# Hybrid decoder step on one core: 20 weight slots in the down products, weight sums and h sums on VectorE

## Chip, cores and metric

One core of a Trainium2 chip. The metric is the device time of one launch in microseconds, lower is better. Times are medians of runs on the chip.

## What is computed

One layer of a hybrid decoder: a prompt of 2048 tokens and 8 single tokens with a paged cache of 8192 past tokens. Attention and a state space model come first, then the gated feed-forward part, which is all that matters here:

```python
xn = rmsnorm(x, p['g_pre_ffn'])
gate = xn @ p['w_gate']                  # 1024 -> 2816
up = xn @ p['w_up']
padded = jnp.concatenate([conv_prev, gate], axis=1)
conv = p['conv_b'] + sum(padded[:, i:i + t] * cw[i] for i in range(3))
hdn = jax.nn.gelu(conv) * up
x = x + rmsnorm(hdn @ p['w_down'], p['g_post_ffn'])   # 2816 -> 1024
```

All values are float32.

## The kernel before, in words

The kernel runs its stages one after another; `stage_ffn` is the last. A float32 product is made of three products of rounded halves: ScalarE rounds an operand to its high part (`split`, `split_wd`, `split_a`), VectorE subtracts to get the low part, TensorE multiplies high by high, high by low and low by high. Large products are made by Strassen's scheme in Winograd's form: seven products (`OPS`, in the order K1, K6, K2, K7, K5, K4, K3) of sums of blocks instead of eight products of blocks.

**The gate loop** (`tiles`) has 44 tiles g: 22 blocks of 128 channels, first for tokens 0 to 1023, then for 1024 to 2047. A tile makes the gate and up values of one block from seven products of 12 matmuls of 128x512 (L2689). Around them in each tile: GpSimd makes four sums of weight blocks for the tile after (`prepare`: L1731, L1733, L1735; `finish`: L1737); ScalarE and VectorE split the seven weight operands of the next tile (L2786, L2938) as soon as TensorE has used the present one; ScalarE copies m1 and one result out of the banks (L2849, L2855) and makes the gelu of the tile before (L2797); VectorE adds the products up (L3025, L3030, L3033, L3036, L3039), makes the convolution (`taps`: L2995, L2998, L2999) and multiplies (L2964), which gives h. In the second half the 8 sample tokens are worked on as well, by small matmuls (L2703, L2711) and small instructions.

TensorE's waits in a tile: product K2 waits for m1 (L2849), K7 for L3025, K4 for L3030, K3 for L3033. All queues are in order, so an instruction that waits holds all that stands behind it on its engine.

The down products use Winograd's form too, so for each pair of tiles GpSimd makes five sums of the blocks of h (`sum_h`: L2594 four, L2596 one), in even tiles, and SyncE stores these and two raw blocks to DRAM (`hop`, L2417). In tiles 4 to 19 the even tiles also do a part of the sums of x for the second half: SyncE loads parts after it has stored h (`load_parts`, L2433), GpSimd makes four sums of them (`sum_parts`, L2605), SyncE stores those. GpSimd's order in an even tile g is: prepare(g+1), sum_h, sum_parts, finish(g+1).

**The down products** are 7 products i of 8 steps u, 56 steps s. A step is 11 x 3 matmuls of 128x512 into one of three banks (L2766): a block of h of 128 tokens (`a`, one 704 KB load, L2474, split by L2822 and L2957, two raw buffers) by the 11 weight operands of the product (`wd`, 16 slots of split operands in the memory of `xw`). A weight operand comes from one or two loads of 256 KB (L2462) into one of three raw slots (`NWD`), the two being added by GpSimd (`sum_wd`, L2638), and is split by L2814 and L2953. A raw slot is loaded again when VectorE has split what it held. Which blocks are loaded is in `PAIRED`; the first product takes two loads for each operand. The operands of product i+1 are loaded and split during the steps of product i, one per step in steps 1 to 5, three in step 6 and the rest in step 7 (`ops_of`). The weights of products 4 and 6 are also used raw for the 8 samples (`sample_down`, L2746), before they are added. Results are copied or added out of the banks by ScalarE (`evacuate`, L2892) and VectorE (`gather`, L3071), and in part copied on by GpSimd (L2665). During products 4 and 6 each step finishes a row of 128 tokens: square (L2900), norm on GpSimd (L2644, L2646), scaling and addition of x on VectorE (L3101, L3104), and the store of y by SyncE. SyncE's order in a step is: the load of h for two steps on, the weight loads, then the store of y, which waits for VectorE.

In the last gate tile (g = 43, `last`) the weight splits of the next tile are replaced by those of the first down product. Its loads start when all gate weights are split (after L2938's last) and the slots allow. Turns of the convolution's tails (L2724) stand behind the first six steps on TensorE.

## Time and profile before

| | us |
|---|---|
| median of 3 runs | 3459.91 (3459.48 to 3466.13) |
| profiled execution | 3459.59 |
| its span, first to last instruction | 3457.6 |
| mean granted clock of TensorE | 0.957 |
| TensorE matmuls busy | 3148.2 (91%) |
| VectorE busy | 2335.3 (68%) |
| ScalarE busy | 1323.6 (38%) |
| GpSimd busy | 1179.2 (34%) |

Busy times are sums over the whole span. Which engine sets the time differs by stage, so the rows that count are those of one stretch: `stage_ffn` begins its matmuls at 1936.9 us. In the trace PE is TensorE's matmuls and PEld its weight loads, DVE is VectorE, ACT ScalarE, POOL GpSimd, SPq the queue of SyncE's transfers. Tile names: `ahead_wf` and `ahead_S` are the raw gate weights and their sums, used again as raw buffers in the down products, `ahead_wop` the split gate weights and later the split h, `ffn_xw` the split x and later the split down weights, `gate_work` the working area of the gate loop, `down_C` the result.

### The profile page before, as it was taken

Reading aid. Unit: us, or ns where it says so; the run is one execution under the profiler, and the core shown is the slowest. Engines: PE = TensorE matmul, PEld = TensorE weight load, DVE = VectorE, ACT = ScalarE, POOL = GpSimd, SP = SyncE. Lnnn points to the kernel's source line nnn. Section 1 sums busy time; section 2 is a strip of 40 time slices with the busy share of each in tenths; the row PEclk is TensorE's granted clock in tenths of the full one; section 3 lists DMA queues with packets and bytes.
Section 4 is the critical chain, followed back from the end, with each engine's and each line's share of the span. In section 5 each row is a group of like instructions: output and inputs, shape, how many; then the busy total and the mean of one; then the engine's idle time right before and its main releaser. Section 6 shows DMA issues by size and latency. Waiting matters only on the chain. (4 is left out here: it accounts for less than half of the span.)

```text
span 3457.6 us, 47005 instructions
## 1 busy us (share of the span) xinstructions
PE 3148.2 (91%) x13945; PEld 2115.6 (61%) x13945; DVE 2335.3 (68%) x2904; ACT 1323.6 (38%) x2249; POOL 1179.2 (34%) x996
## 2 busy tenths in 40 slices
PE   6999985899999999998899599999899998899988
PEld 5787753344444444444787377777677776677666
DVE  6110678987988988994566676667888886344445
ACT  4100113666556556563444332223433332332222
POOL 2000101643444344341144345555355554122112
PEclk9999988999999999999999799999999999999999
DMA  3322234978988988997555233343433334454554
GB/s 116 101 79 67 76 87 118 304 235 281 304 277 284 305 273 288 306 298 242 181 164 151 88 107 105 110 115 109 143 92 96 97 98 126 148 177 163 175 192 167
DMA packets 501235, 591.69 MB, mean 171 GB/s; under 512 B 66191, under 2 KB 308975, under 8 KB 499372
## 3 DMA queue, kind: packets, MB, share of 16 engines
q1 hardware_dynamic: 494094, 574.17, 53.3%
q10 hardware_dynamic: 6912, 15.26, 1.4%
q8 instruction: 75, 1.23, 0.1%
q14 instruction: 122, 1.00, 0.1%
q0 software_dynamic: 32, 0.03, 0.0%
HBM read 484.37 MB, written 103.86 MB: 170 GB/s over the span
## 5 line engine op out<-in xcount | busy, mean ns | idle before, releaser
L2689 PE MATMUL tail_bank<-ffn_xw,ahead_wop 128*128 128x512 f32 x2112 | 530.4, 409 | 72.9 <-DVE ffn_xw L2943 31.6
L2689 PEld LDWEIGHTS tail_bank<-ffn_xw,ahead_wop 128*128 128x128 f32 x2112 | 408.1, 195 | 182.0 <-issue 50.3
L2766 PE MATMUL tail_bank<-ffn_xw,ahead_wop 128*128 128x512 f32 x1848 | 451.0, 405 | 20.8 <-DVE ahead_wop L2957 17.6
L1378 POOL TENSOR_TENSOR att_S<-att_S,att_X 128x512 f32<-128x512 f32 (+3 forms) x256 | 344.7, 1347 | 287.4 <-PE att_bank L1667 216.7
L2766 PEld LDWEIGHTS tail_bank<-ffn_xw,ahead_wop 128*128 128x128 f32 x1848 | 354.7, 193 | 121.1 <-DVE ahead_wop L2957 20.7
L2689 PE MATMUL tail_bank<-gate_xr,ahead_wop 128*128 128x512 f32 x1584 | 381.6, 399 | 16.2 <-DVE gate_work L3030 11.5
L2689 PEld LDWEIGHTS tail_bank<-gate_xr,ahead_wop 128*128 128x128 f32 x1584 | 300.4, 190 | 90.3 <-issue 18.1
L1562 DVE TENSOR_TENSOR att_prod<-att_Kr,att_q_wide 128x1024 f32<-128x1024 f32 x256 | 326.0, 1273 | 5.0 <-DMA att_Kr<-in_cache_k_dram 4.8
L1662 PE MATMUL att_bank<-att_X,att_negtri 128*128 128x512 f32 (+3 forms) x640 | 299.1, 550 | 29.4 <-DVE att_X L1533 28.7
L1567 DVE TENSOR_REDUCE att_z_s<-att_prod 128x16 f32<-128x1024 f32 x256 | 313.3, 1224 | 8.8
L1428 ACT ACTIVATE att_X<-att_bank 128x512 f32<-128x512 f32 (+2 forms) x320 | 171.0, 534 | 257.6 <-PE att_bank L1651 224.3
L1667 PE MATMUL att_bank<-att_S,att_negones 128*128 128x512 f32 (+3 forms) x576 | 259.3, 533 | 0.0
L2786 ACT ACTIVATE ahead_wop<-ahead_wf 128x512 fp32r<-128x512 f32 x215 | 135.2, 629 | 318.6 <-PE tail_bank L2689 218.6
L1436 ACT ACTIVATE att_Wt<-att_bank 128x512 f32<-128x512 f32 (+2 forms) x320 | 168.7, 527 | 128.3 <-PE att_bank L1667 128.0
L1533 DVE SCALAR_TENSOR_TENSOR att_X<-att_X,att_bank 128x512 f32<-128x512 f32 (+2 forms) x320 | 190.9, 598 | 29.7 <-ACT att_X L1430 28.7
L2938 DVE TENSOR_TENSOR ahead_wop<-ahead_wf,ahead_wop 128x512 fp32r<-128x512 f32 x215 | 179.5, 850 | 39.3 <-ACT ahead_wop L2786 37.6
L1374 POOL TENSOR_TENSOR att_S<-att_X,att_zero 128x128 f32<-128x128 f32 x120 | 100.2, 835 | 290.0 <-PE att_bank L1667 178.3
L1651 PEld LDWEIGHTS att_bank<-att_qhh,att_khl 128*128 128x128 f32 x320 | 61.1, 191 | 217.4 <-ACT att_Wt L1436 138.8
L1667 PEld LDWEIGHTS att_bank<-att_S,att_negones 128*128 128x128 f32 x576 | 112.2, 195 | 121.3 <-issue 106.5
L1430 ACT ACTIVATE att_X<-att_X 128x512 f32<-128x512 f32 (+2 forms) x320 | 181.3, 567 | 10.1
L2594 POOL TENSOR_TENSOR gate_work<-gate_work 128x512 f32<-128x512 f32 x88 | 129.1, 1495 | 138.0 <-DVE gate_work L2964 138.0
L1682 PE MATMUL att_bank<-att_Wt,att_vh 128*64 128x512 f32 (+3 forms) x640 | 161.1, 560 | 6.8 <-ACT att_Wt L1436 6.8
(416 smaller groups left out, 5495.9 us busy)
## 6 DMA issues: line engine op xcount, KB each, us to landing
att_Kr<-in_cache_k_dram SPq DMA_DIRECT2D x512, 256.0 KB, 3.7
att_Vr<-in_cache_v_dram SPq DMA_DIRECT2D x488, 256.0 KB, 3.8
hop_dram<-gate_work SPq DMA_DIRECT2D x154, 256.0 KB, 2.6
ahead_wf<-hop_dram SPq DMA_DIRECT2D x56, 704.0 KB, 4.4
ahead_wf<-in_w_gate_dram SPq DMA_DIRECT2D x44, 512.0 KB
ahead_wf<-in_w_up_dram SPq DMA_DIRECT2D x44, 512.0 KB, 5.3
ahead_S<-in_w_down_dram SPq DMA_DIRECT2D x45, 256.0 KB, 4.6
ahead_wf<-in_w_down_dram SPq DMA_DIRECT2D x45, 256.0 KB, 4.6
```

What stands on the lines that cost most here:

```text
L1378: pool.tensor_tensor(new[:, r:], old[:, r:], x[:, r:], ALU.add).then_inc(s_part, 1)
L1428: act.activation(x, bank[:, s % NZ, cols(s):], ACT.Exp).then_inc(e_ready, 1)
L1430: act.activation(x, x, ACT.Ln, bias=1.0).then_inc(l_ready, 1)
L1436: act.activation(Wt[:, u % NW, cols(u):], bank[:, u % NZ, cols(u):], ACT.Exp).then_inc(w_ready, 1)
L1533: stt(x, x, LN_TOP, z, ALU.min, ALU.max).then_inc(sp_ready, 1)
L1562: tt(pr, Kr[:, kk % KSLOTS], q_wide[:, None, :].to_broadcast([P, PP, AW]), ALU.mult).then_inc(k_used, 1)
L1567: dve.tensor_reduce(z_s[:, :, kk * PP:(kk + 1) * PP].rearrange("p h r -> p r h"), prod[:, kk % 2, :].rearrange("p (k h d) -> p k h d", k=P ...
L1662: last = pe.matmul(bank[:, u % NZ, o:], negtri[:], X[:, u % NX, o:], start=False, stop=True, skip_group_check=True)
L1667: last = pe.matmul(bank[:, u % NZ, o2:], negones[:], S[:, (u - 1) % 2, o2:], start=False, stop=True, skip_group_check=True)
L2689: mm = pe.matmul(bank[:, b, :], wop[:, k, w, q], xop(k, x)[:, q], start=(k in (K1, K6, K5) and q == 0 and n == 0), stop=(q == KH - 1 and n ...
L2766: mm = pe.matmul(bank[:, s % 3, :], a_op[s % 2][a][:, p, :], wd_op[:, n % NW, w, :], start=(p == 0 and q == 0), stop=(p == PAIRS_F - 1 and ...
L2938: tt(wop[:, k, 1], weight_part(early, k, s), wop[:, k, 0].bitcast(F32), ALU.subtract).then_inc(w_lo, 1)
```

## The change

All of it is in `stage_ffn` (and `ffn_ahead`, which makes its buffers).

- Memory that held rounded values only is now also seen as raw float32, so that each split weight slot is at the same time the two places of its raw loads: 20 slots (`NW`), loaded in place, summed in place, split in place. The three raw slots are gone. A slot is loaded again when TensorE has used it in the last step of its product.
- Blocks of h have three raw buffers (`NA`) instead of two. The third lies in memory of the gate loop's working area.
- Products 0 and 1 change places: the one with single loads comes first. ScalarE makes two copies of its result (before: one by ScalarE, one by GpSimd).
- The weight sums of the down products go from GpSimd to VectorE, at the end of each step's list. `LOADS`, `SUMS` and `SPLITS` say in which step each operand of the next product is loaded, summed and split.
- VectorE makes the five sums of h of a tile pair, two behind its K2 split and one each behind its splits of K7, K5 and K4; the last pair's stand behind the last multiplication.
- GpSimd makes L1737's sum (`finish`) before `sum_parts`.
- In the last gate tile the splits are placed anew, the first weight operand is loaded a tile earlier, 18 more as the slots come free.

```diff
...
+wd_op = ring_slots(stage_r, early["S_r"], early["wf_r"], xw, wop)
+wd_in = ring_slots(stage, S, wf, xw_raw, early["wop_raw"])
+NW = len(wd_op)
+XW0 = 3
+
+def wd_raw(n, h):
+
+    return wd_in[n % NW][:, 1 - h]
...
-PAIRED = {0: ((0, 1), (1, 1)), 1: ((1, 1),), 2: ((0, 0), (1, 1)), 3: ((1, 0), (0, 0)), 4: ((1, 0), (1, 1)), 5: ((0, 0),), 6: ((0, 0), (0, 1))}
-MINUS = (0, 3)
-NM = OPS * PAIRS_F
+PAIRED = {0: ((1, 1),), 1: ((0, 1), (1, 1)), 2: ((0, 0), (1, 1)), 3: ((1, 0), (0, 0)), 4: ((1, 0), (1, 1)), 5: ((0, 0),), 6: ((0, 0), (0, 1))}
+MINUS = (1, 3)
+LOADS = ((0, 1, 2), (3,), (4, 5), (6,), (7,), (8,), (), (9, 10))
+SUMS = ((), (0, 1), (2,), (3, 4), (5,), (6, 7), (8,), (9, 10))
+SPLITS = ((9, 10), (), (0, 1), (2,), (3, 4), (5,), (6, 7), (8,))
...
-    return range(o + u - 1, o + u) if 1 <= u <= 5 else range(o + 5, o + early_ones) if u == 6 else range(o + late_ones, o + PAIRS_F) if u == 7 else ()
-
-ACT_READS = (1, 1, 0, 1, 0, 0, 0)
+    return tuple((i + 1) * PAIRS_F + p for p in plan[u])
+
+ACT_READS = (2, 1, 0, 1, 0, 0, 0)
...
-            at(sp, wd_lo, n - NWD + 1)
+            if n >= NW:
+                i0, p0 = divmod(n - NW, PAIRS_F)
+                if p0 < PAIRS_F - 1:
+                    sp.wait_ge(wd_used, i0 * (PAIRS_F - 1) + p0 + 1)
+                else:
+                    sp.wait_ge(acc, (i0 + 1) * STEPS)
+            elif n >= XW0:
+                sp.wait_ge(prod, (LASTG - 1) * OPS + min((n - XW0) // 4 + 1 if n < NW - 1 else OPS, OPS))
+            elif n:
+                sp.wait_ge(w_lo, LASTG * OPS)
+                sp.wait_ge(s_made, FT)
+            else:
+                sp.wait_ge(x_ready[K3], 1 + KH)
...
-            at(sp, a_lo, s - 1)
             i, u = divmod(s, STEPS)
-            if s == 4:
-                sp.wait_ge(hraw_stored[0], 16 * 2 * PAIRS_F)
-                sp.wait_ge(hraw_stored[1], 16 * 2 * PAIRS_F)
-                for x in range(4):
-                    sp.wait_ge(hsum_stored[x], 16 * 2 * PAIRS_F * (2 if x == 0 else 1))
-            o = ((i * 2 + u // 4) * 4 + u % 4) * P
-            sp.dma_start(a_raw[s % 2], A["hop"][o:o + P, :]).then_inc(a_loaded[s % 2], 16)
-
-        def body(g):
-            if g < LASTG - 2:
-                weights(g + 2, (g + 2) % FT, g % 2)
-            if g == LASTG - 1:
+            if s < 2:
                 sp.wait_ge(w_lo, LASTG * OPS)
                 sp.wait_ge(s_made, FT)
-                sp.wait_ge(x_ready[K3], 1 + KH)
+            elif s == 2:
+                for done in (c11_ready, c21_ready, c12_ready, saved):
+                    sp.wait_ge(done, LASTG)
+                sp.wait_ge(tapped, LASTG * CW)
+            else:
+                sp.wait_ge(a_lo, s - NA + 1)
...
+            if g == LASTG - 2:
                 load_wd(0)
+            if g == LASTG - 1:
                 load_wd(1)
                 load_a(0)
                 load_wd(2)
                 load_a(1)
-                for n in range(NWD, PAIRS_F):
+                for n in range(XW0, NW - 1):
...
+        load_a(2)
+        load_a(3)
         store_h(LASTG, FT - 2, LASTG % 4, LASTG // 2)
-        sp.wait_ge(h_ready, LASTG)
...
-            if s + 2 < LASTS:
-                load_a(s + 2)
-            for n in ops_of(s, 8, 8):
-                load_wd(n)
+            if 4 <= s + NA < LASTS:
+                load_a(s + NA)
+            for n in ops_of(s, LOADS):
+                if n >= NW - 1:
+                    load_wd(n)
...
-            if j % 2 == 0 and not known(g, 0, 1):
-                sum_h(g, j, h2)
+            if not known(g, LASTG - 1):
+                finish(g + 1, (j + 1) % 2)
             if i is not None and j % 2 == 0:
                 sum_parts(i, j // 2)
-            if not known(g, LASTG - 1):
-                finish(g + 1, (j + 1) % 2)
...
-                    for n in ((0, 1), (2, 3), (4, 5), (6, 7), (8, 9), (10,), ())[k]:
+                    if k == K7:
+                        split_a(0)
+                    for n in ((0, 1), (2,), (3, 4), (5, 6), (7, 8), (9, 10), ())[k]:
                         split_wd(n)
-                    if k == K2:
-                        split_a(0)
-                    if k == K3:
+                    if k == K4:
...
-            dst = {0: C[:, 0, 1, u, :], 1: C[:, 0, 0, u, :], 3: C[:, 1, 0, u, :]}[i]
-            act.activation(dst, bank[:, s % 3, :], ACT.Copy, scale=-1.0 if i == 1 else 1.0).then_inc(c_act, 1)
+            for th, d, sign in {0: ((0, 1, 1.0), (0, 0, -1.0)), 1: ((1, 1, 1.0),), 3: ((1, 0, 1.0),)}[i]:
+                act.activation(C[:, th, d, u, :], bank[:, s % 3, :], ACT.Copy, scale=sign).then_inc(c_act, 1)
...
+        def sum_wd(n):
+
+            i, p = divmod(n, PAIRS_F)
+            if len(PAIRED[i]) == 1:
+                return
+            dve.wait_ge(wd_loaded[n % NW], wd_count(n))
+            if i in SAMPLED:
+                dve.wait_ge(sd_used, sampled_before(n))
+            tt(wd_raw(n, 0), wd_raw(n, 0), wd_raw(n, 1), ALU.subtract if i in MINUS else ALU.add).then_inc(wd_sum, 1)
...
+        def sum_h(g, j, h2, which):
+
+            if which:
+                dve.wait_ge(h_ready, g)
+            e, o = conv[:, (j - 2) % 4], conv[:, (j - 1) % 4]
+            for n in which:
+                x, a, b, op = ((0, e[:, 0:CH], o[:, 0:CH], ALU.add), (1, e[:, CH:], o[:, CH:], ALU.add),
+                               (2, e[:, 0:CH], o[:, CH:], ALU.add), (3, o[:, 0:CH], o[:, CH:], ALU.subtract),
+                               (0, e[:, CH:], e[:, 0:CH], ALU.subtract))[n]
+                at(dve, hsum_stored[x], h2 * 32 - (16 if n == 4 else 32) if x == 0 else h2 * 16 - 16)
+                tt(hsum[:, x, :], a, b, op).then_inc(hsummed, 1)
...
+                    if last:
+                        split_wd(9)
+                        split_wd(10)
+                        split_a(1)
                     taps(g, f, j, h2)
                 if not last:
                     split(g + 1, k, (j + 1) % 2)
                 else:
-                    for n in ((), (0, 1), (2, 3), (4, 5), (6, 7), (8, 9), (10,))[k]:
+                    for n in ((0,), (1, 2), (3,), (4,), (5, 6), (7, 8), ())[k]:
                         split_wd(n)
-                    if k == K7:
+                    if k == K5:
                         split_a(0)
-                    if k == K3:
-                        split_a(1)
                 if k == K6 and not known(g, 0, 1):
                     multiply(g - 1, (j - 1) % 4)
+                if j % 2 == 0 and not known(g, 0, 1):
+                    sum_h(g, j, h2, {K2: (0, 1), K7: (2,), K5: (3,), K4: (4,)}.get(k, ()))
...
+        sum_h(LASTG, LASTG % 4, LASTG // 2, range(5))
...
+            if s % STEPS == 0:
+                for n in ops_of(s, SPLITS):
+                    split_wd(n)
             if s and s + 1 < LASTS:
                 split_a(s + 1)
-            for n in ops_of(s, 0, 5):
-                split_wd(n)
+            if s % STEPS:
+                for n in ops_of(s, SPLITS):
+                    split_wd(n)
             if s and row_of(s - 1) is not None:
                 finish(s - 1)
+            for n in ops_of(s, SUMS):
+                sum_wd(n)
...
```

Lines with "..." stand for parts left out: the buffers' definitions, the same renaming of slots in other places, and the new places of waits that follow from the above.

## Rows read from the trace of the kernel before

**Rows 1.** Stretches: us; busy PE, PEld, DVE, ACT, POOL (xcount); granted clock; DMA share, GB/s
```profile
2060.00:2405.80 345.80, 317.93 (x1300) 253.07 (x1299) 239.34 (x279) 98.77 (x157) 181.37 (x133) 0.96 0.39 109
...
2470.00:2902.10 432.10, 432.10 (x2113) 338.27 (x2112) 356.69 (x470) 137.17 (x243) 223.98 (x134) 1.00 0.33 92
2902.10:2968.30 66.20, 42.91 (x159) 32.20 (x157) 29.54 (x33) 16.17 (x23) 22.54 (x17) 0.81 0.53 171
2968.30:3447.20 478.90, 453.59 (x1884) 345.90 (x1884) 218.54 (x217) 143.39 (x181) 88.64 (x83) 0.97 0.50 173
```

**Rows 2.** Waits, 2060 to 2405.8 us: total us, times, longest
```profile
ACT ahead_wop L2786 <- POOL ahead_wf L1737: 80.4, 8, 10.8
...
PE tail_bank L2689 <- ACT gate_work L2849: 27.9, 8, 4.3
```

**Rows 3.** Timeline, one tile pair of the gate loop: start, us, instruction [idle <-releaser]
```profile
2148.24 5.76 PE L2689 MATMUL tail_bank<-ffn_xw,ahead_wop 128*128 128x512 f32 x24
2157.20 7.42 PE L2689 MATMUL tail_bank<-ffn_xw,ahead_wop 128*128 128x512 f32 x24 [3.19 <-ACT gate_work L2849]
...
2145.46 1.97 SPq L2433 DMA_DIRECT2D ffn_stage<-xnT_dram  x4
...
2149.55 5.22 POOL L2605 TENSOR_TENSOR ffn_stage<-ffn_stage 128x256 f32<-128x256 f32 x4 [4.91 <-DMA ffn_stage<-xnT_dram]
2154.74 1.25 POOL L1737 TENSOR_TENSOR ahead_wf<-ahead_wf,ahead_S 128x512 f32<-128x512 f32 x1
...
2157.30 1.61 POOL L1733 TENSOR_TENSOR ahead_S<-ahead_S,ahead_wf 128x512 f32<-128x512 f32 x1
...
2159.56 1.04 ACT L2797 ACTIVATE gate_work<-gate_work 128x1024 f32<-128x1024 f32 x1
...
2146.31 0.69 DVE L2938 TENSOR_TENSOR ahead_wop<-ahead_wf,ahead_wop 128x512 fp32r<-128x512 f32 x1
...
2161.08 1.22 DVE L2964 TENSOR_TENSOR gate_work<-gate_work 128x1024 f32<-128x1024 f32 x1
```

**Rows 4.** Busy time: odd tile, next even tile, and a pair of the second half
```profile
2148.24:2172.85 24.61, 21.42 (x85) 16.87 (x84) 16.41 (x18) 6.23 (x10) 15.75 (x12) 0.93 0.25 72
2172.85:2192.50 19.65, 19.65 (x86) 15.87 (x85) 14.56 (x18) 6.36 (x10) 7.61 (x6) 1.00 0.59 163
...
2626.20:2668.60 42.40, 42.40 (x209) 33.20 (x208) 34.98 (x46) 13.56 (x24) 22.01 (x13) 1.00 0.34 93
```

**Rows 5.** Chain that ended last, in order: start, us, what
```profile
2959.14 6.12 DMA ahead_wf<-hop_dram
2965.28 1.39 ACT ahead_wop L2822
2966.69 1.64 DVE ahead_wop L2957
...
3003.28 69.31 PE tail_bank L2766 x297
...
3165.73 0.98 PE tail_bank L2746 x4
```

**Rows 6.** Timeline of the turn from gate to down products
```profile
2926.78 5.46 PE L2689 MATMUL tail_bank<-gate_xr,ahead_wop 128*128 128x512 f32 x12 [10.51 <-DVE gate_work L3030]
...
2967.18 1.02 PE L2724 MATMUL tail_bank<-kept_ident,ffn_tails 128*10 128x128 f32 x4 [7.38 <-ACT down_C L2911]
...
2911.44 1.30 POOL L2638 TENSOR_TENSOR ahead_S<-ahead_S 128x512 f32<-128x512 f32 x1 [10.56 <-DMA ahead_S<-in_w_down_dram]
```

**Rows 7.** Waits of the down products, 2968.3 to 3447.2 us
```profile
PE tail_bank L2766 <- DVE ahead_wop L2957: 17.6, 7, 4.4
```

**Rows 8.** Groups by line, second half: xcount | busy, mean ns | idle before
```profile
L2938 DVE TENSOR_TENSOR ahead_wop<-ahead_wf,ahead_wop 128x512 fp32r<-128x512 f32 x102 | 75.2, 752 | 1.2
L2594 POOL TENSOR_TENSOR gate_work<-gate_work 128x512 f32<-128x512 f32 x42 | 61.7, 1497 | 36.3 <-DVE gate_work L2964 36.3
```

**Rows 9.** Page, slices of the span: what the DMA moved
```profile
GB/s 116 101 79 67 76 87 118 304 235 281 304 277 284 305 273 288 306 298 242 181 164 151 88 107 105 110 115 109 143 92 96 97 98 126 148 177 163 175 192 167
```

More of the change, by code:

```diff
@@ L1708, in ffn_ahead @@
     m = Stage(nc, ctx, "ahead")
+    with ExitStack() as rounded:
+        mr = Stage(nc, rounded, "rounded")
+        wf_r = mr.far("wf", [P, 2, 4, KH, P], F32R)
+        S_r = mr.far("S", [P, 2, KH, P], F32R)
+        wop = mr.far("wop", [P, OPS, 2, KH, P], F32R)
     wf = m.far("wf", [P, 2, 4, KH, P])
     S = m.far("S", [P, 2, KH, P])
-    wop = m.far("wop", [P, OPS, 2, KH, P], F32R)
+    wop_raw = m.far("wop_raw", [P, OPS, 2, KH, P])
     prm = m.far("prm", [P, FT, ROWS])
@@ L2244, in stage_ffn @@
         st = m.sb("st", [P, 3, 2])
+        with ExitStack() as rounded:
+            mr = Stage(nc, rounded, "rounded")
+            stage_r = mr.sb("stage", [P, 2, CH], F32R)
+            xw = mr.sb("xw", [P, 4, 2, KH, CH], F32R)
         stage = m.sb("stage", [P, 2, CH])
-        xw = m.sb("xw", [P, 4, 2, KH, CH], F32R)
+        xw_raw = m.sb("xw_raw", [P, 4, 2, KH, CH])
         with ExitStack() as gates:
@@ L2266, in stage_ffn, with ring_slots @@
         raw = wf[:].rearrange("p s q k c -> p (s q k c)")
-        S_raw = S[:].rearrange("p s k c -> p s (k c)")
-        AW1 = PAIRS_F * P
-        a_raw = [raw[:, n * AW1:(n + 1) * AW1] for n in range(2)]
-        wd_raw = [S_raw, raw[:, 2 * AW1:2 * AW1 + 2 * CH].rearrange("p (s n) -> p s n", s=2), stage[:]]
-        NWD = len(wd_raw)
+        NA = 3
+        a_raw = [raw[:, 0:AW1], raw[:, AW1:2 * AW1], a_far[:]]
         ring = wop[:].rearrange("p o h k c -> p (o h k c)")
         a_op = [[ring[:, (2 * n + h) * AW1:(2 * n + h + 1) * AW1].rearrange("p (f t) -> p f t", t=P) for h in range(2)] for n in range(2)]
-        wd_op = xw[:].rearrange("p o h k n -> p (o h k n)").rearrange("p (w h n) -> p w h n", h=2, n=CH)
-        NW = 16
+        halves = lambda x: x.rearrange("p (h n) -> p h n", h=2)
+        def ring_slots(first, second, third, most, end):
+            flat = most[:].rearrange("p o h k n -> p (o h k n)")
+            return ([first[:], halves(second[:].rearrange("p s k c -> p (s k c)")),
+                     halves(third[:].rearrange("p s q k c -> p (s q k c)")[:, 2 * AW1:2 * AW1 + 2 * CH])]
+                    + [halves(flat[:, x * 2 * CH:(x + 1) * 2 * CH]) for x in range(16)]
+                    + [halves(end[:].rearrange("p o h k c -> p (o h k c)")[:, 4 * AW1:4 * AW1 + 2 * CH])])
+        wd_op = ring_slots(stage_r, early["S_r"], early["wf_r"], xw, wop)
[4 more added lines that the diff above has]
+            return wd_in[n % NW][:, 1 - h]
         def xop(k, h):
@@ L2382, in samples_of @@
         def samples_of(i, where):
-            return {**{u: (u - 2,) for u in range(2, 7)}, 7: (5, 6, 7), 8: (8, 9, 10)}.get(where, ()) if i + 1 in SAMPLED else ()
+            return ((), (0, 1), (2,), (3, 4), (5,), (6, 7), (8,), (), (9, 10))[where] if i + 1 in SAMPLED else ()
         def sampled_before(n):
@@ L2483, in body @@
+                    if s == 0:
                         for x in range(2):
@@ L2765, in _ @@
                         for q, (a, w) in enumerate(((0, 0), (0, 1), (1, 0))):
-                            mm = pe.matmul(bank[:, s % 3, :], a_op[s % 2][a][:, p, :], wd_op[:, n % NW, w, :], start=(p == 0 and q == 0),
+                            mm = pe.matmul(bank[:, s % 3, :], a_op[s % 2][a][:, p, :], wd_op[n % NW][:, w], start=(p == 0 and q == 0),
                                            stop=(p == PAIRS_F - 1 and q == 2), skip_group_check=True)
```

110 lines of the change are left out of this document (46 added, 64 removed).

## The prediction

> **What bounds the kernel now.** Everything the change touches lies in the last stage, from 1937 us on, so I read the busy times by stretch first [rows 1]. The second half of the gate loop is full: 432.1 us busy out of 432.1. TensorE sets its pace and nothing taken off another engine shortens it; an engine that becomes too full lengthens it. Time is lost in three places. The first half of the gate loop has 317.9 of 345.8 us busy, at a granted clock of 0.96. The turn from gate to down products takes 66.2 us with TensorE busy for 42.9. The down products take 478.9 us.
>
> **First place, the gate loop.** The waits say who is late [rows 2]: TensorE waits 27.9 us in 8 pieces for ScalarE's copy on L2849, and ScalarE stood 80.4 us in 8 pieces behind GpSimd's L1737, the fourth weight sum. The timeline of one of the eight tile pairs shows the path [rows 3]: GpSimd makes its sums of h, waits 4.9 us for the x parts that SyncE could only fetch after the last sum of h was stored, works on them for 5.2 us (L2605), and only then makes L1737, at 2154.7. ScalarE's queue is in order, so the copy of m1 behind it is late and TensorE stands for 3.19 us. That tile lasts 24.6 us against 19.65 us for the next one [rows 4]: 5.0 us lost, of which 1.8 us are slower matmuls, since the granted clock was 0.93 in that tile and 1.00 in the next; matmuls go at the lower of the two levels (1.2 instead of 2.4 GHz) for a while after the standstill.
>
> **Second place, the turn.** From 2902.1 to 2968.3 one gate tile (19.65 us) and two down steps are done. A down step is 69.31/9 = 7.70 us for 33 matmuls [rows 5], 8.05 with a turn of the tails, an estimate. 19.65 + 2 x 8.05 = 35.7, so 30.5 us are lost. The standstills are 10.51 us for L3030 on VectorE and 7.38 us near the end [rows 6]. Both come from three raw weight slots: each holds two loads, GpSimd adds them (first sum at 2911.4, after 10.56 us of waiting for the DMA), ScalarE and VectorE split them, and their own gate work stands behind those splits. The last chain [rows 5] is a late load of h: GpSimd's last sums of h, then 6.12 us of DMA, 1.39 and 1.64 us of splits.
>
> **Third place, the down products.** 54 steps x 7.70 = 415.8 us and 22 groups of sample products x 0.98 = 21.6 us [rows 5] make 437.4 of the 478.9 us [rows 1]; 41.5 us are lost. 17.6 us are standstills before the split of h (L2957), up to 4.4 us each [rows 7]; the rest is waits for weights, and matmuls slowed after these (granted clock 0.97).
>
> **The change, part by part.**
> *Sums of h on VectorE.* Removed from GpSimd: 5 per tile pair at 1.50 us [rows 8]. Added to VectorE: 5 at 0.69 to 0.75 us, taken from its split of the same size and operand count [rows 3, 8]; 3.5 to 3.8 us per pair. In a pair of the second half VectorE is busy 35.0 of 42.4 us [rows 4], so 7.4 us are free, and the five are spread over four places where it waits for TensorE. I cost them at nothing there; if that cover were gone they would be 22 x 3.8 = 84 us.
> *The fourth weight sum ahead of the x parts.* L1737 no longer waits behind L2605, so the wait of 3.19 us before K2 goes. What is late next: the sums of tile g+2, still behind L2605. The fifth sum of h now comes after VectorE's K4 split, which ends at 2147.0, so at 2147.7, and the x parts are asked for at about 2148.5 instead of 2145.5. L2605 ends near 2157.8 instead of 2154.8. Two weight sums more (2.9 us, the end of L1733 less the end of L1737) give 2160.8; ScalarE's split (0.63) and gelu (1.04), VectorE's product L2964 (1.22), its split (0.69) and the addition L3030 (0.69) follow in order and end near 2165.0. TensorE wants that addition for K4 at 2148.24 + 5 x 2.8 = 2162.2. So it stands about 2.5 us in a new place. With slower matmuls behind it I take 4.0 us per pair against 5.0: 8 x 1.0 = **8 us** gained. The ends are 0 and 5.0 us of loss per pair.
> *The turn.* The first down product now uses single loads that need no sum, 19 slots can be asked for during the last gate tile, and the first is asked for one tile earlier. 10 x 256 KB and 2 x 704 KB are 4.0 MB; the kernel got 171 GB/s on average in this stretch [rows 1], but with slots blocked. The highest slice of the whole span moved 308 GB/s [rows 9]; with requests close together I take that, 13 us, from 2907 to about 2921; at 171 GB/s it would be 24 us. By VectorE's order the splits, the gelu of tile 42 and its product then hold back K4 by about 2 us, and the first step begins near 2924 instead of 2940. Its two steps end near 2941. The third wants a block of h whose load waits for VectorE's last taps (2932): 6.1 us of DMA [rows 5], more behind the weights; and VectorE's five last sums now stand ahead of that split in its queue, the fifth waiting for the store of the first. I put the third step at 2945 against 2968.4: **23 us**. Ends: 15 and 30.5.
> *Down products.* The 55 weight sums cost GpSimd no time that shows; on VectorE they are 44 x 0.75 = 33 us beside 218.5 us busy in 478.9 [rows 1], 7 points more. What matters is order: a weight is asked for two steps ahead of its split, and a third slot for h takes L2957's loads off SyncE's stores of y. A split of h takes 1.39 + 1.64 us [rows 5] of a 7.70 us step. The standstills should go, all but sample groups, turns of the tails and a slow start after the turn; I leave 9.5 us: **32 us**. Ends: 15 and 41. The second copy out of the bank on ScalarE (0.6 us, 8 times, for GpSimd's copy) lies under a step.
>
> The sum is 8 + 23 + 32 = 63 us. The profiled execution took 3459.6 us (span 3457.6 and 2.0 around it), 0.3 us below the median of the runs, so this is 3459.6 - 63 = **3397 us** on either.
>
> **A rule against the change.** Splits on VectorE with two inputs from SBUF take 0.69 us in one tile [rows 3] and 0.75 us on average in the second half [rows 8]: little is lost there to GpSimd's sums. The Trainium skill ("SBUF — State Buffer", section "SBUF: two separate sides") says that such a VectorE instruction and a GpSimd instruction that reads SBUF exclude each other for the whole instruction. By that, every moved sum that meets a GpSimd sum costs its length more; what that would make of the time is rival 3. The average above agrees with it only if such meetings are rare or short.
>
> **The rivals.**
> 1. *The gate loop's standstill goes altogether*, if the x parts arrive as early as before or the chain to K4 is shorter: 8 x 5.0 = 40 instead of 8 us, 3365 us. For it: 2.5 us is a small margin. Against: L2605 still precedes the sums. 0.10.
> 2. *Half comes back*: VectorE, now with sums that wait for DMA and sample products in one in-order queue, holds TensorE at each of the six changes of product and in the turn. Half of 55 us: 3425 us. For it: this queue had no weight sums before. Against: it is under two thirds busy. 0.17.
> 3. *Slower: VectorE bounds the gate loop.* Price: a sum that meets a GpSimd sum costs 0.75 + 1.5 = 2.25 us, five are 11.2 us where 7.4 are free, 3.8 us over, x 22 = 84 us; 3397 + 84 = 3481 us. It decides from (7.4 + 63/22)/5 = 2.1 us per sum on. Against: GpSimd's own sums fall in a pair to 9 instead of 14 instructions, and the measured 0.75 us. 0.05.
> 4. *The change does not do what it says*: the turn and the down products are limited by the DMA, so that earlier requests end no earlier. Only the loop's 8 us stay: 3452 us. The DMA share of 0.50 to 0.53 [rows 1] speaks against it. 0.06.
>
> **How the numbers follow.** My forecast has 0.62, from 3382 to 3412 by its ends taken partly together. With half of rival 2 and most of the space to rival 1 the range is 3372 to 3425. 0.2% (7 us) is what a measurement can tell. Faster: all but rival 3 and stray mishaps, 0.93; same 0.02; slower 0.05.
>
> **What would show it.** Gate loop: TensorE's wait moves from L2849 to VectorE's L3030, 2 to 3 us, eight times; L1737 no longer waits behind L2605. Second half: still 432 us, all busy, VectorE near 90%. Turn: no 10.5 us standstill; the third step near 2937, as everything is 8 us earlier. Down: no waits over 2 us before L2957, clock 1.00 after the first steps. A second half above 435 us would make the prediction wrong on VectorE; a wait before weights at changes of product would be rival 2.

## The result, and the profile of the changed kernel

The median of four runs is **3365.3 us** (3362.5 to 3369.3) against 3459.7 for the kernel before on the same chip, a ratio of 0.9725 (95% interval 0.9708 to 0.9742): faster by 94 us. The prediction said faster, by 63 us, at 3397; its range ended at 3372, so the time lies 7 us outside, on the fast side. The profiled execution took 3369.3 us (span 3367.6) and is the longest of the four. Against the profiled execution of before that is 90 us less, and the stages ahead of the feed-forward part take 5.7 us more of it in this trace (its first matmuls start at 1942.6, before at 1936.9), so the last stage alone gains 95.7.

The stretches of the last stage, to be laid beside [rows 1] and [rows 4] (us; busy PE, PEld, DVE, ACT, POOL; granted clock; DMA share, GB/s): a tile pair of the gate loop's first half and its odd tile, the whole first half, the second half and one pair of it, the turn, the down products from their third step on.

```profile
2079.22:2120.43 41.21, 39.43 (x169) 31.50 (x169) 31.22 (x42) 12.36 (x20) 15.31 (x13) 1.00 0.44 122
2104.49:2125.90 21.41, 19.63 (x85) 15.56 (x84) 14.54 (x18) 6.01 (x10) 12.29 (x10) 1.00 0.40 111
2060.00:2405.80 345.80, 328.84 (x1415) 261.82 (x1413) 260.15 (x340) 101.51 (x165) 127.10 (x99) 1.00 0.43 120
2429.30:2880.30 451.00, 447.44 (x2184) 349.60 (x2185) 384.94 (x546) 145.40 (x258) 155.78 (x84) 1.00 0.34 95
2604.80:2647.20 42.40, 42.40 (x212) 33.16 (x208) 36.16 (x52) 13.48 (x25) 14.84 (x8) 1.00 0.34 93
2880.31:2922.36 42.05, 37.78 (x160) 29.64 (x158) 28.88 (x39) 17.91 (x26) 0.00 (x0) 0.96 0.81 279
2922.36:3357.04 434.68, 434.67 (x1884) 336.63 (x1884) 241.62 (x270) 140.97 (x186) 20.26 (x32) 1.00 0.56 189
```

With the same marks in both traces, the account of the last stage is:

| from | before, us | after, us | gained | predicted |
|---|---|---|---|---|
| first matmul to the first tile of the second half | 513.8 | 486.7 | 27.1 | 8 |
| from there to the last gate tile | 451.4 | 451.1 | 0.4 | 0 |
| last gate tile to the third down step | 66.3 | 42.1 | 24.2 | 23 |
| third down step to the last matmul | 478.8 | 434.7 | 44.1 | 32 |

The last matmul ends at 3357.0, the span 10.6 us later (before 10.4). Two terms stand out: the gate loop gave three times what was predicted, the down products 12 us more. In the rows above, the first half of the gate loop runs at a granted clock of 1.00, where before it was 0.96, and the down products have TensorE busy for all of their 434.7 us.

The waits of TensorE in the first half, beside [rows 2], say where the loop now waits: not on ScalarE's copy, but on VectorE's L3063, the addition before K4 (L3030 in the old lines).

```profile
ACT rounded_wop L2798 <- POOL ahead_S L1738: 60.0, 8, 7.5
...
PE tail_bank L2701 <- DVE gate_work L3063: 14.0, 8, 1.8
```

Eight waits, 14.0 us, 1.8 at most. The timeline of one pair, beside [rows 3] (start, us, instruction, idle before and its releaser), shows the path to one of them:

```profile
2104.64 1.96 SPq L2460 DMA_DIRECT2D ffn_stage<-xnT_dram  x4
...
2108.86 4.53 POOL L2642 TENSOR_TENSOR ffn_stage<-ffn_stage 128x256 f32<-128x256 f32 x4 [11.68 <-DMA ffn_stage<-xnT_dram]
...
2114.73 1.29 POOL L1738 TENSOR_TENSOR ahead_S<-ahead_S,ahead_wf 128x512 f32<-128x512 f32 x1
...
2116.13 0.63 ACT L2798 ACTIVATE rounded_wop<-ahead_S 128x512 fp32r<-128x512 f32 x1 [7.52 <-POOL ahead_S L1738]
2116.67 1.04 ACT L2809 ACTIVATE gate_work<-gate_work 128x1024 f32<-128x1024 f32 x1
...
2117.87 1.21 DVE L2985 TENSOR_TENSOR gate_work<-gate_work 128x1024 f32<-128x1024 f32 x1
...
2119.61 0.67 DVE L3063 TENSOR_TENSOR gate_work<-gate_work,tail_bank 128x512 f32<-128x512 f32 x1
...
2120.43 1.87 PE L2701 MATMUL tail_bank<-gate_xr,rounded_wop 128*128 128x512 f32 x7 [1.78 <-DVE gate_work L3063]
```

It is the chain that the prediction wrote down, link by link: x parts asked for late, GpSimd's four sums of them, two weight sums, ScalarE's split and gelu, VectorE's product and addition. The x parts take 4.53 us, not 5.22. It holds TensorE for 1.78 us where 2.5 were expected, and the matmuls behind it keep the clock: all eight groups of 24 take 5.83 or 5.84 us, where the 24 behind the old wait took 7.42 [rows 3].

The turn, beside [rows 6]:

```profile
2896.58 7.38 PE L2701 MATMUL tail_bank<-gate_xr,rounded_wop 128*128 128x512 f32 x24 [2.11 <-DVE gate_work L3063]
...
2922.36 0.97 PE L2778 MATMUL tail_bank<-rounded_stage,rounded_wop 128*128 128x512 f32 x3 [2.15 <-DVE rounded_wop L2978]
...
2913.38 2.50 DVE L2997 TENSOR_TENSOR gate_work<-gate_work 128x512 f32<-128x512 f32 x4
2920.07 0.69 DVE L2997 TENSOR_TENSOR gate_work<-gate_work 128x512 f32<-128x512 f32 x1 [4.19 <-DMA hop_dram<-gate_work]
2920.68 1.62 DVE L2978 TENSOR_TENSOR rounded_wop<-down_a_far,rounded_wop 128x1408 fp32r<-128x1408 f32 x1
```

The waits of 10.51 and 7.38 us are two of 2.1 us. The first of them, 2.11 us, is followed by the slower matmuls (24 in 7.38 us instead of 5.84; the stretch has a granted clock of 0.96), so in the turn this kernel does lose the clock, behind a wait only 0.3 us longer than those of the loop. The second is VectorE's split of h (L2978) behind its fifth sum of h, which waited 4.19 us for the store of the first. After that step TensorE has no wait in the down products at all [rows 7 of before had 17.6 us].

### The profile page after: what moved, and what is told of

It is laid out like the page before. It is cut to its first block and busy times, and to the rows that moved or that the text cites. A ratio compares the mean times of both kernels' runs of the same rounds, so it can differ in the third digit from the quotient of the medians.

```text
span 3367.6 us, 46986 instructions
## 1 busy us (share of the span) xinstructions
PE 3115.7 (93%) x13945; PEld 2096.1 (62%) x13945; DVE 2377.6 (71%) x3069; ACT 1320.8 (39%) x2257; POOL 931.9 (28%) x823
## 5 line engine op out<-in xcount | busy, mean ns | idle before, releaser
L2701 PE MATMUL tail_bank<-rounded_xw,rounded_wop 128*128 128x512 f32 x2112 | 515.4, 401 | 44.3 <-DVE rounded_xw L2954 31.4
L2701 PEld LDWEIGHTS tail_bank<-rounded_xw,rounded_wop 128*128 128x128 f32 x2112 | 398.6, 191 | 148.0 <-issue 50.1
L2701 PE MATMUL tail_bank<-gate_xr,rounded_wop 128*128 128x512 f32 x1584 | 380.8, 397 | 18.5 <-DVE gate_work L3063 17.2
L2778 PE MATMUL tail_bank<-rounded_xw,rounded_wop 128*128 128x512 f32 x1488 | 357.3, 396 | 0.0
L2701 PEld LDWEIGHTS tail_bank<-gate_xr,rounded_wop 128*128 128x128 f32 x1584 | 297.9, 189 | 94.4 <-DVE rounded_wop L2949 17.3
L2778 PEld LDWEIGHTS tail_bank<-rounded_xw,rounded_wop 128*128 128x128 f32 x1488 | 278.3, 188 | 77.9 <-issue 11.7
L2798 ACT ACTIVATE rounded_wop<-ahead_wf 128x512 fp32r<-128x512 f32 x215 | 134.2, 628 | 264.5 <-PE tail_bank L2701 235.7
L2949 DVE TENSOR_TENSOR rounded_wop<-ahead_wf,rounded_wop 128x512 fp32r<-128x512 f32 x215 | 157.3, 747 | 12.8 <-ACT rounded_wop L2798 11.4
L1651 PE MATMUL att_bank<-att_qhh,att_khl 128*128 128x512 f32 (+2 forms) x320 | 156.4, 489 | 1.4 <-ACT att_Wt L1436 0.8
```

The source lines that it names most:

```text
L1651: mm = pe.matmul(bank[:, s % NZ, o:], key[:, j * P:(j + 1) * P], part[:, c * CH + o:(c + 1) * CH], start=(q == 0), stop=(q == 1))
L2701: mm = pe.matmul(bank[:, b, :], wop[:, k, w, q], xop(k, x)[:, q], start=(k in (K1, K6, K5) and q == 0 and n == 0), stop=(q == KH - 1 and n ...
L2778: mm = pe.matmul(bank[:, s % 3, :], a_op[s % 2][a][:, p, :], wd_op[n % NW][:, w], start=(p == 0 and q == 0), stop=(p == PAIRS_F - 1 and q ...
```

## The experiments

Kernels e1 to e4 shared one chip, e5 to e8 another, e9 to e12 a third; ratios are to the kernel before on the same chip. Edits are to the changed kernel unless another is named. "Sums of h on GpSimd" are made there as in the kernel before. Line numbers shift by a few from one kernel to the next.

**Which part brings the gain.** The change mixes three things that touch the gate loop or the down products: the slots with all that belongs to them, the place of the sums of h, and the place of L1742 (L1737 in the old lines) before or after the x parts. The first three kernels take the combinations that the change left out.

e1_form_only, the slots and weight sums of the change, with sums of h and order as before:

```diff
-                    if not known(g, LASTG - 1):
-                        finish(g + 1, (j + 1) % 2)
+                    if j % 2 == 0 and not known(g, 0, 1):
+                        sum_h(g, j, h2)
                     if i is not None and j % 2 == 0:
                         sum_parts(i, j // 2)
+                    if not known(g, LASTG - 1):
+                        finish(g + 1, (j + 1) % 2)
...
-                        if j % 2 == 0 and not known(g, 0, 1):
-                            sum_h(g, j, h2, {K2: (0, 1), K7: (2,), K5: (3,), K4: (4,)}.get(k, ()))
```

> The changed kernel with GpSimd making the five sums of h again and L1737 again behind the work on the x parts (prepare, sums of h, x parts, L1737): only slots, weight sums and their placing are left of the change. Theory: the gate loop's share (27 us between the traces) hangs on these two edits alone, the turn's 24 us and the down products' 44 us do not. So the loop pair is 44.3 us again with the 3.2 us standstill on the copy of m1 and a granted clock under 1.00, and the time is 3365 + 26 = 3391 us. Rival: part of the loop's gain comes from the slots or the build as a whole; then under 3380.

Measured: 3386.8 us, ratio 0.9791 (0.9772 to 0.9809). e2_order_only, the same with `finish` ahead of `sum_parts`:

> As the run before, but with L1737 right behind GpSimd's sums of h and ahead of the x parts. Theory: the order alone takes the standstill away; with the sums on GpSimd the x parts are asked for some 3 us earlier than with the sums on VectorE, the weight sums of the tile after end some 3 us earlier, and the 1.76 us standstill before K4 is not there either: 8 x 1.76 = 14 us faster than the changed kernel, 3351 us, loop pair 39.2 us. Then moving the sums to VectorE costs time. Rival: the sums on VectorE are what pays; then the loop stands as before, 3391 us.

Measured: 3355.4 us, 0.9697 (0.9678 to 0.9716), below the changed kernel. e3_sums_only, the changed kernel with `finish` behind `sum_parts` again:

> The changed kernel with sums of h on VectorE, but L1737 again behind the x parts. Theory: the x parts come about 3 us later than with the sums on GpSimd and L1737 with them, so the standstill on the copy of m1 grows from 3.2 to about 6 us with slower matmuls behind it: 8 x 3 us slower than with both on GpSimd, 3415 us (3405 to 3425). Rival: GpSimd relieved of 7.2 us per pair makes L1737 in time; then 3365 to 3380 us.

Measured: 3410.1 us, 0.9859 (0.984 to 0.9878). The three rows of TensorE's waits in the first half (2060 to 2400 us), one of each kernel, tell why:

```profile
PE tail_bank L2715 <- ACT gate_work L2866: 28.4, 8, 4.3
```
```profile
PE tail_bank L2715 <- DVE gate_work L3077: 3.3, 8, 1.0
```
```profile
PE tail_bank L2701 <- ACT gate_work L2852: 38.3, 8, 4.9
```

e1 has the old wait on the copy of m1; e2, with the order alone, keeps 3.3 us of waits; e3, with the sums alone, has a longer wait on the copy than before, since the x parts are asked for after VectorE's last sum. So the order is what takes the loop's wait away. Moving the sums of h to VectorE costs 23 us without the order (e3 less e1). With it the cost is less sure: changed less e2 is 10 us, but the two were not run side by side, their intervals overlap, and the changed kernel once more (e12, below) had 0.9705, 0.0008 above e2. What speaks for a cost are the profiles: a pair of e2's loop lasts 40.2 us against 41.2, and its stretch from the last gate tile to the last matmul 472.3 against 476.7, together 8 + 4.4 us.

One after the other, by the ratios: slots, weight sums and placing alone gain 72 us (e1), the order 33 more (e2), and the sums of h take some 10 back, which leaves the 95 that the change has by its ratio. What within the 72 is due to the 20 slots, to the exchange of products 0 and 1 or to the places of loads and splits was not tried apart.

**The order alone, on the kernel before.** e9_before_order_only puts L1737 ahead of the x parts in the old kernel and changes nothing else:

```diff
                         sum_h(g, j, h2)
+                    if not known(g, LASTG - 1):
+                        finish(g + 1, (j + 1) % 2)
                     if i is not None and j % 2 == 0:
                         sum_parts(i, j // 2)
-                    if not known(g, LASTG - 1):
-                        finish(g + 1, (j + 1) % 2)
```

> The kernel before with one edit: L1737 right behind GpSimd's sums of h and ahead of the x parts. Theory: the loop's share does not hang on slots or on VectorE. The 3.2 us standstill goes, some tenths remain as in the form with this order (loop pair 40.2 instead of 44.3 us): 8 x 4.1 = 33 us faster, 3427 us, ratio 0.990. Rival: the gain needs the relieved GpSimd; then no change.

Measured: 3430.1 us, 0.9904 (0.9883 to 0.9926), 33 us by the ratio. So 33 of 94 us are to be had by moving one call. Its waits, beside [rows 2]:

```profile
PE tail_bank L2689 <- DVE gate_work L3030: 3.3, 8, 1.0
PE tail_bank L2689 <- DVE gate_work L3025: 1.5, 7, 0.3
```

**How long a standstill the clock bears.** My forecast had 2.5 us with slower matmuls behind them; the trace has 1.78 at full clock. To see whether the length alone decides, GpSimd makes one more sum of weights of the odd tiles, between its x parts and L1736: half a block in e5, a whole one in e6, so that the same chain ends later.

```diff
+                    if i is not None and j % 2 == 1:
+                        pool.wait_ge(w_lo, g * OPS + K5 + 1)
...
+                        tt(S[:, 0, 0:2], wfx[:, A21, 0:2], wfx[:, A22, 0:2], ALU.add).then_inc(dup, 1)
+                        pool.wait_ge(dup, i * 2 - 1 + j // 2)
                     if not known(g, LASTG - 1):
                         prepare(g + 1, (j + 1) % 2, h2 + j % 2)
```

> The changed kernel with one more GpSimd instruction of 128x256 ahead of the sums that the K4 standstill hangs on, in the eight tile pairs. It lengthens that standstill from 1.76 to about 2.4 us, near the 2.5 us of the prediction. Theory: below the 3.2 us of the kernel before TensorE's clock is not lowered, so only the wait itself is added: 8 x 0.65 = 5 us, 3370 us, granted clock 1.00 in the loop. Rival: 2.4 us is enough, as the prediction took it; then each pair loses 1.7 us more, 3384 us, clock 0.96.

> The same with 128x512: the standstill grows to about 3.05 us. Theory: near enough to 3.2 us that the clock falls for a while in most pairs, 8 x (1.3 + 1.7) = 24 us, 3389 us. Rival: the clock holds, 3376 us.

Measured: e5 3383.3 us, 0.9775 (0.9758 to 0.9791); e6 3391.5 us, 0.9798 (0.9782 to 0.9815). Two neighbouring waits of e5, and one of e6 (24 matmuls after each wait):

```profile
2164.15 7.38 PE L2709 MATMUL tail_bank<-gate_xr,rounded_wop 128*128 128x512 f32 x24 [2.66 <-DVE gate_work L3071]
2207.79 5.84 PE L2709 MATMUL tail_bank<-gate_xr,rounded_wop 128*128 128x512 f32 x24 [2.66 <-DVE gate_work L3071]
```
```profile
2159.47 7.38 PE L2709 MATMUL tail_bank<-gate_xr,rounded_wop 128*128 128x512 f32 x24 [3.22 <-DVE gate_work L3071]
```

The same 24 matmuls last 5.84 us at full clock and 7.38 when it falls. In e5 the waits are 2.66 to 2.99 us and five of the eight are followed by the longer time; in e6 they are 3.22 to 3.48 and all eight are. In the loop of the changed kernel, at 1.72 to 1.78 us, none is, nor in its repetition e12; in e4 and in e8, both below, one of eight each, at 1.79. Between 1.8 and 2.1 us there are single waits only: 1.88 us in e2's turn and 2.06 in e8's loop are not followed by the longer time, 1.93 in e3's turn, 1.99 in e1's and 2.11 in the changed kernel's are; in e12 this wait of the turn is 1.75 us and the time 5.83. So e5's theory, that only the wait is added (3370 us), was wrong, and its rival's 3384 came out.

A pair of e5 lasts 42.98 us on average over seven, one of the changed kernel 41.18: 1.8 us more per pair, 0.9 of it wait and the rest slower matmuls. That is 14 us for eight pairs; e5 less changed is 18 us by the medians, not run side by side. Two full tiles are 39.3 us (2 x 19.65), so e5 loses 3.7 us per pair, where the prediction took 4.0 for a wait of 2.5 us. Its price was about right for its wait; the wait was not there.

**Does VectorE have room?** e7_sums_twice makes each sum of h twice on VectorE, 3.45 us more per pair where 6.2 us look idle in a pair of the second half.

```diff
+                        tt(hsum[:, x, :], a, b, op).then_inc(dup, 1)
+                        dve.wait_ge(dup, h2 * 5 - 4 + n)
                         tt(hsum[:, x, :], a, b, op).then_inc(hsummed, 1)
```

> The changed kernel with each of VectorE's five sums of h made twice: 3.45 us more per tile pair. Theory: VectorE still has room (36.2 of 42.4 us busy in a pair of the second half), so the second half stays full and the time grows only where a sum is on the path: the fifth sum and with it the x parts come 0.7 us later in eight pairs, and some in the turn, 3370 to 3380 us. Rival (the prediction's third): VectorE bounds the gate loop; then TensorE stands in the second half and the time is over 3400 us.

Measured: 3427.0 us, 0.9901 (0.9885 to 0.9918). I had expected no loss in the second half; this missed by 50 us. A pair there, in the windows view; then TensorE's three waits in it, and one doubled sum (L2998 and L3000) beside GpSimd's:

```profile
2624.11:2669.17 45.06, 43.01 (x209) 33.09 (x209) 39.37 (x57) 13.55 (x24) 14.51 (x8) 1.00 0.32 88
```
```profile
2624.11 1.07 PE L2716 MATMUL tail_bank<-ahead_wf,ffn_xs 128*32 128x256 f32 x16 [1.49 <-DVE ffn_hs L3097]
...
2661.32 3.04 PE L2702 MATMUL tail_bank<-gate_xr,rounded_wop 128*128 128x512 f32 x12 [0.27 <-DVE gate_work L3066]
2664.64 3.04 PE L2702 MATMUL tail_bank<-gate_xr,rounded_wop 128*128 128x512 f32 x12 [0.28 <-DVE gate_work L3069]
```
```profile
2656.86 0.68 DVE L2998 TENSOR_TENSOR gate_work<-gate_work 128x512 f32<-128x512 f32 x1
2657.01 1.69 POOL L1742 TENSOR_TENSOR ahead_wf<-ahead_wf,ahead_S 128x512 f32<-128x512 f32 x1 [4.24 <-DVE rounded_wop L2950]
2657.57 1.68 DVE L3000 TENSOR_TENSOR gate_work<-gate_work 128x512 f32<-128x512 f32 x1
```

A pair takes 45.06 us instead of 42.40 while VectorE is busy for 39.4, and all three waits of TensorE, 2.0 us together, are for VectorE. So here VectorE's queue sets the pace at 87% busy. My reading is that its idle time lies ahead of instructions that wait for TensorE, so that work added in other places pushes back what TensorE waits for; that was not tried by moving the added sums elsewhere. In any case the 6 us of idle time were no measure of what could be added.

**Weight sums of the down products.** e4_wd_on_gpsimd makes them on GpSimd, all else as changed:

```diff
                     if s and row_of(s - 1) is not None:
                         finish(s - 1)
-                    for n in ops_of(s, SUMS):
-                        sum_wd(n)
...
                         norm(row_of(s - 1))
+                    for n in ops_of(s, SUMS):
+                        sum_wd(n)
```

> The changed kernel with the weight sums of the down products on GpSimd, slots and steps unchanged. Theory: slots and distance make the gain, not the engine: the sums have two steps of room, so 3365 us within 5. Rival: GpSimd's sums (1.3 us and more against 0.7) and its norms in one queue bring waits for weights back; then 3375 us or more, with standstills in the steps of products 4 and 6.

Measured: 3374.6 us, 0.9751 (0.9733 to 0.9768). In the profiles the last gate tile to the last matmul takes 481.8 us against 476.7, and nearly all of the difference (4.8 of 5.1 us) lies in the turn; from the third step on e4 has no wait either. So 3374.6 came out at the rival's time, but not by its mechanism, standstills in products 4 and 6. The turn's timeline:

```profile
2903.78 11.23 POOL L2672 TENSOR_TENSOR ffn_xw_raw<-ffn_xw_raw 128x512 f32<-128x512 f32 x6 [1.06 <-DMA ffn_xw_raw<-in_w_down_dram]
...
2906.08 2.71 DVE L2980 TENSOR_TENSOR rounded_wop<-ahead_wf,rounded_wop 128x1408 fp32r<-128x1408 f32 x1
...
2911.73 4.36 DVE L3033 SCALAR_TENSOR_TENSOR gate_work<-gate_work,ahead_prm 128x1024 f32<-128x1024 f32 x2
...
2916.22 1.02 PE L2748 MATMUL tail_bank<-kept_ident,ffn_tails 128*10 128x128 f32 x4 [7.03 <-DVE ffn_tails L3034]
```

In the changed kernel, where GpSimd does nothing in this stretch, the split of h takes 1.62 us and the two taps 2.60:

```profile
2905.81 1.62 DVE L2978 TENSOR_TENSOR rounded_wop<-ahead_wf,rounded_wop 128x1408 fp32r<-128x1408 f32 x1
...
2908.40 2.60 DVE L3031 SCALAR_TENSOR_TENSOR gate_work<-gate_work,ahead_prm 128x1024 f32<-128x1024 f32 x2
```

Six sums of GpSimd side by side with VectorE's last taps make both slower (1.87 us each for GpSimd's, 1.3 elsewhere), and TensorE waits 7.0 us for the tails. By the rule that the prediction weighed (the Trainium skill, "SBUF — State Buffer", section "SBUF: two separate sides"), a VectorE instruction with two inputs from SBUF and a GpSimd instruction that reads SBUF exclude each other for the length of an instruction. These rows fit it: 2.71 and 4.36 us against 1.62 and 2.60, which is 1.1 us more for the split and 0.9 for each tap, beside sums of 1.3 to 1.9 us.

**The third buffer of h.** e8_two_h_buffers sets `NA = 2` and drops the waits for the third buffer's memory.

```diff
-        NA = 3
+        NA = 2
```

> The changed kernel with two raw buffers for blocks of h instead of three. Theory: the gain of the down products comes from weights asked for two steps ahead, and with these no load waits long in SyncE's queue, so the third buffer is worth under 5 us: 3360 to 3370 us (the third block comes earlier in the turn, since it no longer waits for the taps: up to 2 us of gain). Rival: it is the third buffer that takes the loads of h off the stores of y; then the 12 us of standstills of product 4 return, 3378 us or more.

Measured: 3369.5 us (3362.0 to 3376.0), 0.9739 (0.9721 to 0.9757): no difference that could be told. The third buffer is worth nothing that shows here; with two, the profile has no wait before the third step and the down products run as full. With e4, where GpSimd makes the weight sums and they run as full too, this leaves the slots and the placing of loads and splits as what fills the down products: an argument by elimination.

**Can the rest of the loop's wait be had?** The x parts are asked for behind the stores of h, which now wait for VectorE's last sum. In e10 and e11 SyncE asks for them ahead of these stores; e11 has the sums of h on GpSimd as e2.

```diff
+                            load_parts(i, j // 2)
                             store_h(i * 4 + j, None, j, i * 2 + j // 2)
-                            load_parts(i, j // 2)
```

> The changed kernel with SyncE asking for the x parts ahead of its stores of h. Theory: what is left in the loop is GpSimd's work on the x parts standing ahead of the next tile's sums because the parts come late; asked for early it is done in the even tile, and the 1.76 us standstill goes: 8 x 1.76 = 14 us, 3351 us. Rival: it then runs beside VectorE's sums of h and holds these up; then 3358 us or more, with new waits in the even tiles.

> Slots and order of the change, sums of h on GpSimd (as the second run), and the x parts asked for ahead of the stores of h. Theory: the last 0.5 us of standstill and the slowed instructions per pair go, loop pair 39.2 us: 8 x 1.0 = 8 us faster than the second run, 3347 us, about 3% under the kernel before. Rival: GpSimd is full in these tiles, nothing changes, 3355 us.

e12_changed_again is the changed kernel on that chip:

> The changed kernel once more, beside the other three on the same chip: 3365 us, ratio 0.9725. By the theory the second run's form is 0.0028 below it, which is then no difference between chips.

Measured: e12 3363.6 us, 0.9705 (0.9687 to 0.9723); e10 3356.0 us, 0.9677 (0.9658 to 0.9696), 7.6 less than e12, where the theory had 14 and the rival 7 at most; e11 3364.2 us, 0.971 (0.9689 to 0.973), where 3347 was expected. In e10 a pair lasts 39.9 us against 41.2:

```profile
2070.86:2110.72 39.86, 39.43 (x168) 31.50 (x169) 32.62 (x42) 12.98 (x21) 15.36 (x12) 1.00 0.44 126
```

In e11 it lasts 41.0, though its chain over the x parts is gone. Its timeline:

```profile
2140.44 1.74 POOL L1736 TENSOR_TENSOR ahead_S<-ahead_wf 128x512 f32<-128x512 f32 x1
2141.17 4.32 DVE L3045 SCALAR_TENSOR_TENSOR gate_work<-gate_work,ahead_prm 128x1024 f32<-128x1024 f32 x2
...
2142.25 2.16 POOL L1738 TENSOR_TENSOR ahead_S<-ahead_S,ahead_wf 128x512 f32<-128x512 f32 x1
2144.49 2.15 POOL L1740 TENSOR_TENSOR ahead_wf<-ahead_wf 128x512 f32<-128x512 f32 x1
2145.41 1.26 DVE L3046 TENSOR_SCALAR ffn_tails<-gate_work 128x2 f32 x1
...
2147.78 0.68 DVE L3072 TENSOR_TENSOR gate_work<-gate_work,tail_bank 128x512 f32<-128x512 f32 x1
2148.61 3.03 PE L2715 MATMUL tail_bank<-rounded_xw,rounded_wop 128*128 128x512 f32 x12 [1.63 <-DVE gate_work L3072]
...
2162.15 2.71 DVE L3045 SCALAR_TENSOR_TENSOR gate_work<-gate_work,ahead_prm 128x1024 f32<-128x1024 f32 x2
```

GpSimd, free earlier, makes its three weight sums exactly while VectorE makes its taps: 4.32 us instead of the 2.71 of the next tile, the small instruction behind them takes 1.26 us, the addition before K7 is late, and TensorE waits 1.6 us. As the timeline reads, the gain of one wait was paid for by a collision that had not been there; e11 equals e12 on the same chip. In e10 the same three sums lie ahead of the taps, which VectorE, with its sums of h, begins later:

```profile
2142.89 1.62 POOL L1740 TENSOR_TENSOR ahead_wf<-ahead_wf 128x512 f32<-128x512 f32 x1
```
```profile
2145.87 2.71 DVE L3031 SCALAR_TENSOR_TENSOR gate_work<-gate_work,ahead_prm 128x1024 f32<-128x1024 f32 x2
```

The last of them ends at 2144.5, and the taps take their 2.71 us.

The best versions are e2 (3355.4 us, 0.9697) and e10 (3356.0, 0.9677); the changed kernel had 0.9725 and 0.9705. All five runs of e10 are shorter than all five of e12 on the same chip. The intervals of the ratios overlap, and no run of the changed kernel stands beside e2; the profiles show the shorter pairs in both.

## Why the prediction was wrong in size, and where it was right

- **Right: what bounds the three places, and that all three open.** Signs, causes and the new last links were as written: L3030's addition in the loop, the fifth sum before the split of h in the turn, nothing in the second half (0.4 us).
- **The step that failed: "With slower matmuls behind it I take 4.0 us per pair against 5.0".** The new wait was sized 2.5 us and priced as one at which the clock falls. It is 1.78 us at a granted clock of 1.00. A pair lasts 41.2 us, before 44.3 (24.61 + 19.65, [rows 4]) to 44.4 in other pairs: 3.2 us per pair instead of 1.0, eight times that is 25 us, and about 2 more lie at the ends of the stretch. So the loss is 1.9 us per pair where I had 4.0: 0.7 of the difference is the wait itself, 1.4 the slower matmuls that did not come. The links of my chain as written end at 2165.0 where 2162.2 was wanted, 2.8 us and not 2.5. Of these, 0.7 are the x parts' 5.22 us, which I took from one timeline of the kernel before and which are 4.53 in the new place (why was not tried), and 0.3 the two weight sums, 2.9 us taken and 2.7 measured (2113.35 to 2116.02), with smaller differences. The price is not linear in that error: by e5's trace, a wait 0.9 us longer costs 1.8 us per pair. The estimate stood where a longer or a shorter wait decides over the clock, and I gave one side the whole weight. Rival 1, "the standstill goes altogether, 3365 us", was right by its time alone, and by luck: 14 us of waits stay, the loop gave 27 us and not 40, and the down products the other 12.
- **Down products: 44 instead of 32 us.** I left 9.5 us over a floor of 437.4, for a slow start, sample groups and tails; no such loss shows, and the granted clock is 1.00 from the third step on. The floor itself was 2.7 us too high, because I took 22 groups of four sample matmuls at 0.98 us, 21.6 us. The trace has these 88 matmuls in 14 rows, seven of them with eight matmuls in about the time of four, 14.9 us by the starts of the rows behind them:

```profile
3251.04 1.07 PE L2758 MATMUL tail_bank<-ffn_xw_raw,ffn_hs 128*32 128x512 f32 x8
...
3259.91 1.05 PE L2758 MATMUL tail_bank<-ffn_xw_raw,ffn_hs 128*32 128x512 f32 x4
```

  The kernel before has such rows of eight too, but only two of them (3368.89 is one, 1.05 us). What makes two groups run together was not tried.
- **Turn: 24.2 instead of 23 us.** The first down step began 23.5 us after the last gate tile (2903.8 less 2880.3), where 2924 less 2902.1 = 21.9 was predicted; the core moved 279 GB/s on average over the turn, where I took 308 for its loads. The third step waits for the fifth sum, as written, and began 42.05 us after the tile where 42.9 was predicted, so two misses cancel in part.
- **"I cost them at nothing" for the sums of h** held in the second half, not in the rest: their move costs 23 us without the order (e3 less e1), and with it about 10 (changed less e2, with the doubt given there). They make the x parts late (through the stores) and hold the split of h in the turn. I had both mechanisms in the sum, and did not see that they made this part of the change a loss. Each sum was also dearer than the 0.69 to 0.75 us that I took from the split, 0.86 on average in the second half, so 4.3 us per pair instead of 3.5 to 3.8:

```profile
L2997 DVE TENSOR_TENSOR gate_work<-gate_work 128x512 f32<-128x512 f32 x55 | 46.6, 863 | 0.0
```

- **Rival 3, VectorE as the bound,** was not what happened, but its point of decision was put too far off. I counted 7.4 us of room in a pair and 2.1 us per sum as where it decides; the change used some of that room without a loss, but by e7 another 3.45 us already cost 2.7 us per pair.
- Rivals 2 and 4 fell: there is no wait before weights at changes of product, and the turn moved 279 GB/s where it had moved 171 and ended 24 us sooner, so earlier requests did end earlier.

## What to carry to other kernels

Do not price a standstill of TensorE by a line: it costs its own length, and here 1.5 us of slower matmuls on top where the clock falls. If an estimate falls among lengths at which the runs show both outcomes, give each a case of its own. When an instruction in an in-order queue is late because it stands behind work that nobody waits for as urgently, move it first: on the kernel before, one moved call gave 33 us. And before work is moved between VectorE and GpSimd, look at what each end triggers: what is asked for behind it, and what it will then run beside.

## What the runs showed of the hardware

- The fall of the clock after a wait isn't sharp. Waits of TensorE ahead of 24 such matmuls, and how many were followed by a time of 7.1 us or more instead of 5.84: none of sixteen at 1.72 to 1.78 us (the loops of the changed kernel and e12); one of eight each in the loops of e4 and e8, at 1.79, but not e8's longest of 2.06; in the turns of e1 to e3 two of three, at 1.93 and 1.99 and not at 1.88; in the turns of the changed kernel, e6, e8 and e10 all four, at 2.11, 2.19, 2.40 and 2.60; five of eight in e5, at 2.66 to 2.99; all eight in e7, at 2.65 to 3.14; all eight in e6's loop, at 3.22 and over. The same kernel had both outcomes at the same 2.66 us, so the length of the wait alone doesn't decide.
- VectorE with operands in SBUF, beside GpSimd: taps 1.36 us each in a tile where the weight sums lie elsewhere, 2.16 beside them (e11); a sum of 128x512 0.68 and 1.68; the split of 128x1408 1.62 and 2.71; even an instruction on 128x2 took 0.16 alone and 1.26 beside them. GpSimd's own sums went from 1.3 to 2.2 us. It is the tiny ones that surprise: the one on 128x2 loses 1.1 us, nearly the length of a GpSimd sum alone.
